# A Strassen projection in another order, with four of seven low halves of weights on GpSimd instead of five

## The chip, the cores and the metric

The kernel runs on one core of a Trainium2 chip. The metric is the time of one execution on the device in microseconds (us); smaller is better.

## The reference

One encoder layer over two sequences of 1024 and 512 tokens, 1536 in all, with 1024 channels, in float32. What the change touches is the first step, the projection of the normalised input to all branches:

```python
h = _rmsnorm(x, norm_pre)
p = h @ w_in
idx = [int(i) for i in np.cumsum(SPLIT_SIZES)[:-1]]
q_m, k_m, v_m, o_m, z_m, if_raw, q_a, k_a, v_a, z_a, g_m, g_a = jnp.split(p, idx, axis=-1)
```

`w_in` has 1024 rows and 9744 columns. The mLSTM branch, the grouped attention branch with a two-dimensional rotary embedding (rope) on q and k, the gates and the output projection follow.

## The kernel before

Four functions run one after the other, each behind a barrier of all engines: `project`, `attend`, `mlstm` and `finish`. Only `project` (from line 270) and the tables in front of it (lines 108 to 268) are touched.

**Products.** Float32 is multiplied as two parts of fp32r, high and low: hi x hi + hi x lo + lo x hi, three matmuls for each slice of 128 channels (lines 1063 to 1065). The matrix product is done by Strassen's scheme, in Winograd's form: activations and weights are cut in four blocks, and seven products of sums of blocks (A11, A12, S2, S3, S1, A22, S4, in this order) give the four corners. The tokens are done in two passes of 768. In each, 19 units of 512 columns of weights follow one another; a unit in a pass is called a run, 38 in all: 9 of a pass write p by tokens (three tiles of 256 columns to a product, four of them with gates, whose two halves are multiplied after sigmoid and silu), 10 by features (two tiles of 384 tokens). The first run of a pass is 8 columns wider, for the input and forget gates.

**One product.** SyncE loads the weights of a run in two halves (`raw`, three buffers). VectorE makes the weights' sums, called rest: S3 (line 725), S2 (731), S1 (733, in place) and A22 (737, in place). ScalarE rounds each to its high half (942, a ring of three slots, which waits until the product three before has ended), and GpSimd (611) or VectorE (741) subtracts it for the low half: GpSimd for A11, A12, S3, S1 and S4, VectorE for S2 and A22. TensorE multiplies tile by tile into one of two groups of three PSUM banks; before a product it waits until all of the product two before is evacuated. Each tile is evacuated by itself: A11 by ScalarE (948), the others by VectorE (752, 757, 771, 773), which adds it to what it has of the scheme in `parts` and writes corners to `stage`. ScalarE applies the gates' functions (953) and issues the stores. VectorE waits for the store of the run before ahead of the first tile of a corner.

**Activations.** Before a pass the input's tiles are normalised (ScalarE 918 and 923, VectorE 698, 704 and 708), the sums S1 to S4 are made by GpSimd (622 to 627) into one buffer `sums`, and 21 blocks of 128 tokens a pass are transposed by TensorE ("flip", 1039), rounded by ScalarE (929) and their low halves made by VectorE (715). In the first pass the flips are ordered by tile of tokens, then by block, and the last ones stand ahead of product S2 or S3 of run 0. For the second pass this work is laid between the products of runs 15 to 18, by way of DRAM.

**Rope.** While later units are multiplied, 12 tiles of q and k (six in runs 3 to 14, six in runs 22 to 35) are loaded, squared, normalised, turned by cosine (VectorE, 875) and sine (GpSimd, 646: four instructions), added (885), multiplied by the norm on GpSimd (653), split in high and low (ScalarE 1002 to 1004, VectorE 889 to 893), transposed on TensorE (1089) and copied out of PSUM alternately by ScalarE (1011) and VectorE (900).

**Order.** `project_plan` (line 172) gives every step a tick, where one tick is the time of one product; run r begins at tick 7r. Each engine takes its steps strictly in the order of their ticks, and semaphores alone make it wait:

```python
def at(engine, tick, kind, *n):
    plan[engine].append((tick, len(plan[engine]), kind, n))
```

The function `over_turns` and the product helper of line 101 belong to other stages.

Of the kernel before, what the change touches and what calls it, by code (L numbers as in the profile page):

```python
# [125 lines left out]
POOL_LOWS = (A11, A12, S3, S1, S4)  # L126
# [38 lines left out]
def flip_order():  # L165

    order = [(0, b, j) for j in range(HTT) for b in (A11, A12)]
    order += [(0, b, j) for j in range(HTT) for b in (S2, S3, S1, A22, S4)]
    return order + [(1, b, j) for b in range(PRODUCTS) for j in range(HTT)]


def project_plan():
# [17 lines left out]
    for j in range(HTT):  # L190
# [24 lines left out]
    for r in range(RUNS):  # L215
# [5 lines left out]
        at("dve", start - 0.9, "rest", r, S3)  # L221
        at("dve", start - 0.6, "rest", r, S2)
        at("dve", start + 1.2, "rest", r, S1)
        at("dve", start + 2.3, "rest", r, A22)
        n = HTT if tokens else 2
        for b in range(PRODUCTS):
            q = start + b
            at("act", q - 1.95, "high", r, b)
            at("pool" if b in POOL_LOWS else "dve", q - 1.6, "low", r, b)
            for i in range(n):  # L230
                at("pe", q + i / n, "product", r, b, i)
                at("act" if b == A11 else "dve", q + (i + 1) / n + 0.05, "out", r, b, i)
            if b in CORNERS:
                if funcs[0] is not ACT.Copy:
                    at("act", q + 1.3, "shape", r, b)
                if gated and b >= A22:
                    at("dve", q + 1.6, "gate product", r, b)
                if b >= A22:
                    at("act", q + (1.9 if gated else 1.4), "send", r, b)
# [11 lines left out]
    for t in range(TT):  # L251
        p = t // (2 * HTT)
        base, pace = ROPE_BASE[p] + ROPE_PACE[p] * (t % (2 * HTT)), ROPE_PACE[p] / 12
        for engine, tick, kind in (
                ("sp", 0.3, "load tile"), ("dve", 1.5, "tables"), ("act", 1.6, "rope square"), ("dve", 2.0, "sum squares"),
                ("act", 2.4, "rope root"), ("dve", 2.5, "cosine"), ("pool", 2.5, "sine"), ("dve", 2.9, "invert"),
                ("dve", 3.6, "add"), ("pool", 4.0, "rope normalise"), ("act", 4.7, "rope high"), ("dve", 5.4, "rope low"),
                ("sp", 6.3, "store v")):
            at(engine, base + pace * tick, kind, t)
        for f in range(RBANKS):  # L260
            tick = base + pace * (6.6 + 0.75 * f)
            at("pe", tick, "rope transpose", t, f)
            at("dve" if f % 2 else "act", tick + 0.3 * pace, "rope empty", t, f)
# [6 lines left out]
def project(nc, x, w_in, norm_pre, b_if, rope, q_gain, k_gain, p_feat, p_tok, stacks, v_stacks, neg_max, columns, bounce,  # L270
            blocks):

    with Scope(nc, "a") as sc:
# [15 lines left out]
        def room(first, *shape):  # L289
# [30 lines left out]
        acc = [[sc.pb(f"acc{g}{i}", [P, CH]) for i in range(HTT)] for g in range(2)]  # L320
# [4 lines left out]
        squared, mean_made, root_made, rstd_made, h_made, sums_made = (sc.sem(n) for n in (  # L325
            "squared", "mean_made", "root_made", "rstd_made", "h_made", "sums_made"))
# [39 lines left out]

        def unit_of_run(r):
# [11 lines left out]
        tiles_until = [sum(tiles(i) for i in range(r)) for r in range(RUNS + 1)]  # L379
# [8 lines left out]
        def full_count(r, b, i):  # L388
            return PRODUCTS * tiles_until[r] + b * tiles(r) + i + 1

        def out_count(r, b, i):

            if b == A11:
                return out_act, CREDIT + tiles_until[r] + i + 1
            return out_dve, CREDIT + (PRODUCTS - 1) * tiles_until[r] + (b - 1) * tiles(r) + i + 1

        def await_out(eng, r, b, i=None):
            eng.wait_ge(*out_count(r, b, tiles(r) - 1 if i is None else i))

        def low_count(r, b):  # L400

            mine = POOL_LOWS if b in POOL_LOWS else (S2, A22)
# [37 lines left out]
        def bank(r, b, i):  # L440
            return acc[(PRODUCTS * r + b) % 2][i]

        def part_of(which, r, i):

            w = width(r)
            return parts[:, which, i * w:(i + 1) * w]

        def place(r, b, i=None):

            lower_tokens, lower_cols = {A12: (True, True), S1: (False, False), A22: (False, True), S4: (True, False)}[b]  # L450
            if unit_of_run(r)[0]:
                s, edge_at = 0 if lower_tokens else 1, HALF - narrow(r) // 2
                cut = slice(0, edge_at) if lower_cols else slice(edge_at, 2 * HALF)
                v = stage[:, s, :].rearrange("p (n c) -> p n c", c=2 * HALF)[:, :, cut]
            else:
                s = 0 if lower_cols else 1
# [1779 lines left out]
```

## Time and profile before

| What | us |
|---|---|
| Median of three runs (2544.54 to 2550.89) | 2549.8 |
| The profiled execution, own time | 2546.88 |
| Its span from first to last instruction | 2544.8 |
| First product of the projection begins | 33.5 |
| Run 1 begins | 88.9 |
| Last matmul of the projection ends | 1319.4 |
| PE busy over the span (91%) | 2316.1 |
| DVE busy (65%) | 1657.7 |
| ACT busy (48%) | 1211.0 |
| POOL busy (45%) | 1139.5 |

In the profile PE is TensorE, PEld its load of weights, DVE VectorE, ACT ScalarE, POOL GpSimd and SP SyncE. Names of tiles carry the stage as first letter (`a_` is the projection), L and a number is a line of the kernel. Times in a trace count from the span's start. Matmuls overlap in their records, so the pace of PE is read from how many stand in a window, not from the mean duration of one. The clock in a window is the share of full speed granted to TensorE. A wait is idle time of an engine, with the instruction that ended it.

### The profile page before, as it was taken

The numbers are of one execution on the slowest core, as the hardware profiler recorded it, in microseconds if no ns is written. First come the engines' busy times: TensorE is split into PE (matmuls) and PEld (weight loads), VectorE is DVE, ScalarE is ACT, GpSimd is POOL, SyncE is SP. The second block draws the span as 40 slices with busy tenths as digits, with TensorE's granted clock in tenths as the row PEclk, the third lists the DMA queues.
The fourth block names the chain that finished last, engine by engine and source line by source line (L and its number), as shares of the span: only waits on it lengthen the run. The fifth ranks groups of instructions, "written<-read, shape, count | busy, mean of one in ns | idle before, by whom it ended". The sixth has DMA issues, their size and how long they took to land. (4 is left out here: it accounts for less than half of the span.)

```text
span 2544.8 us, 38884 instructions
## 1 busy us (share of the span) xinstructions
PE 2316.1 (91%) x14261; PEld 2121.3 (83%) x14261; DVE 1657.7 (65%) x2583; ACT 1211.0 (48%) x1976; POOL 1139.5 (45%) x626
## 2 busy tenths in 40 slices
PE   4999989998999999999978998989869995999998
PEld 4999989998899999999977777777668884888887
DVE  5567777765666778777638888888768872113222
ACT  4233553343443355334427877878667873211121
POOL 3454445545434544554426776767600002534420
PEclk9999999999999999999989999999989997999999
DMA  2334434455543333444424332221054434753332
GB/s 109 118 130 134 133 119 143 157 170 187 187 141 135 130 113 129 156 155 159 145 107 137 106 98 88 87 87 38 17 164 154 149 100 160 254 173 104 120 141 83
DMA packets 203462, 331.93 MB, mean 130 GB/s; under 512 B 10288, under 2 KB 96144, under 8 KB 203280
## 3 DMA queue, kind: packets, MB, share of 16 engines
q1 hardware_dynamic: 177712, 275.57, 33.4%
q10 hardware_dynamic: 25568, 54.01, 5.5%
q8 instruction: 104, 1.70, 0.3%
q14 instruction: 78, 0.64, 0.1%
HBM read 223.18 MB, written 106.37 MB: 129 GB/s over the span
## 5 line engine op out<-in xcount | busy, mean ns | idle before, releaser
L611 POOL TENSOR_TENSOR a_w_lo<-a_raw,a_w_hi 128x1024 fp32r<-128x1024 f32 (+1 forms) x152 | 397.7, 2619 | 364.2 <-ACT a_w_hi L942 364.2
L1063 PE MATMUL a_acc<-a_w_hi,a_act_hi 128*128 128x256 f32 (+1 forms) x1512 | 438.0, 290 | 26.6 <-DVE a_stage L771 11.7
L1064 PE MATMUL a_acc<-a_w_lo,a_act_hi 128*128 128x256 f32 (+1 forms) x1512 | 432.8, 286 | 0.0
L1065 PE MATMUL a_acc<-a_w_hi,a_act_lo 128*128 128x256 f32 (+1 forms) x1512 | 432.6, 286 | 0.0
L1063 PE MATMUL a_acc<-a_act_hi,a_w_hi 128*128 128x384 f32 x1120 | 386.1, 345 | 38.8 <-POOL a_w_lo L611 14.4
L942 ACT ACTIVATE a_w_hi<-a_raw 128x1024 fp32r<-128x1024 f32 (+1 forms) x190 | 201.5, 1061 | 423.6 <-PE a_acc L1065 381.8
L1065 PE MATMUL a_acc<-a_act_hi,a_w_lo 128*128 128x384 f32 x1120 | 379.3, 339 | 0.0
L1064 PE MATMUL a_acc<-a_act_lo,a_w_hi 128*128 128x384 f32 x1120 | 378.7, 338 | 0.0
L1763 POOL TENSOR_TENSOR t_prob<-t_prob,t_rsum 128x1024 f32<-128x1024 f32 (+1 forms) x192 | 308.2, 1609 | 124.2 <-DVE t_rsum L1783 124.1
L1063 PEld LDWEIGHTS a_acc<-a_w_hi,a_act_hi 128*128 128x128 f32 x1512 | 294.5, 195 | 30.1 <-issue 21.3
L771 DVE TENSOR_TENSOR a_stage<-a_parts,a_acc 128x256 f32<-128x256 f32 (+3 forms) x376 | 172.8, 471 | 225.0 <-PE a_acc L1065 201.7
L1064 PEld LDWEIGHTS a_acc<-a_w_lo,a_act_hi 128*128 128x128 f32 x1512 | 294.6, 195 | 0.0
L1065 PEld LDWEIGHTS a_acc<-a_w_hi,a_act_lo 128*128 128x128 f32 x1512 | 294.4, 195 | 0.0
L1063 PEld LDWEIGHTS a_acc<-a_act_hi,a_w_hi 128*128 128x128 f32 x1120 | 213.6, 191 | 46.1 <-issue 27.6
L2066 POOL TENSOR_TENSOR f_w_lo<-f_raw,f_w_hi 128x512 fp32r<-128x512 f32 x48 | 63.7, 1357 | 358.7 <-ACT f_w_hi L2082 358.7
L1779 DVE TENSOR_REDUCE t_nmax<-t_scr 128x1 f32<-128x1024 f32 (+1 forms) x192 | 199.2, 1037 | 34.2 <-PE t_scr L1842 34.1
L1789 DVE TENSOR_TENSOR t_pt_lo<-t_flip,t_pt_hi 128x512 fp32r<-128x512 f32 x320 | 206.7, 679 | 18.2 <-issue 10.6
L1064 PEld LDWEIGHTS a_acc<-a_act_lo,a_w_hi 128*128 128x128 f32 x1120 | 214.2, 191 | 0.0
L1065 PEld LDWEIGHTS a_acc<-a_act_hi,a_w_lo 128*128 128x128 f32 x1120 | 213.5, 191 | 0.0
L1810 ACT ACTIVATE t_prob<-t_scr,t_nmax 128x1024 f32<-128x1024 f32 (+1 forms) x192 | 187.5, 977 | 48.6 <-DVE t_nmax L1779 32.7
L1842 PE MATMUL t_scr<-t_k,t_q 128*128 128x512 f32 x640 | 184.1, 402 | 28.7 <-DMA t_k<-stacks 19.2
L611 POOL TENSOR_TENSOR a_w_lo<-a_rest,a_w_hi 128x1024 fp32r<-128x1024 f32 (+1 forms) x38 | 96.9, 2550 | 248.8 <-ACT a_w_hi L942 248.7
(214 smaller groups left out, 5168.6 us busy)
## 6 DMA issues: line engine op xcount, KB each, us to landing
a_raw<-w_in SPq DMA_DIRECT2D x56, 1024.0 KB, 5.3
p_feat<-a_stage ACTq DMA_DIRECT2D x40, 768.0 KB, 3.5
stacks<-a_guest SPq DMA_DIRECT2D x72, 256.0 KB, 2.6
a_raw<-w_in SPq DMA_DIRECT2D x32, 512.0 KB, 4.7
p_tok<-a_stage ACTq DMA_DIRECT2D x20, 768.0 KB, 3.5
t_q<-stacks SPq DMA_DIRECT2D x8, 1536.0 KB, 6.6
t_k<-stacks SPq DMA_DIRECT2D x16, 768.0 KB, 9.1
m_raw<-p_feat SPq DMA_DIRECT2D x24, 512.0 KB, 4.0
```

The source lines that it names most:

```text
L611: nc.gpsimd.tensor_sub(slot_of(w_lo, r, b), weights_of(r, b), slot_of(w_hi, r, b).bitcast(F32))\
L771: ins = nc.vector.tensor_add(out, known[:, skip:w], a[:, skip:w])
L942: nc.scalar.activation(slot_of(w_hi, r, b), weights_of(r, b), ACT.Copy).then_inc(hi_made, 1)
L1063: nc.tensor.matmul(out, s_hi, m_hi, start=begin, stop=False)
L1064: nc.tensor.matmul(out, s_hi, m_lo, start=False, stop=False)
L1065: last = nc.tensor.matmul(out, s_lo, m_hi, start=False, stop=end)
L1763: nc.gpsimd.tensor_mul(prob[n % 3][:, 0:w], prob[n % 3][:, 0:w], rsum[:, 1, n % 4:n % 4 + 1].to_broadcast([P, w])).then_inc(normed, 1)
L1779: nc.vector.tensor_reduce(out=nmax[:, n % 4:n % 4 + 1], in_=scr[n % 2][:, 0:w], axis=AX.X, op=ALU.max, negate=True).then_inc(max_made, 1)
L1789: nc.vector.tensor_sub(pt_lo[b][place(m, i)], flip[x % FLIPS][:], pt_hi[b][place(m, i)].bitcast(F32)).then_inc(lo_made[x % FLIPS], 1)
L1810: nc.scalar.activation(prob[n % 3][:, 0:w], scr[n % 2][:, 0:w], ACT.Exp, bias=nmax[:, n % 4:n % 4 + 1], accum_out=rsum[:, 0, n % 4:n % 4 + ...
L1842: ins = nc.tensor.matmul(scr[n % 2][:, i * CH:(i + 1) * CH], q_t[s][:, hd % 2, q * P:(q + 1) * P], k_t[s][:, part, keys], start=(part == 0 ...
L2066: nc.gpsimd.tensor_sub(w_lo[cut], raw[:, k % (KT // 2), :], w_hi[cut].bitcast(F32))\
```

## The change

- GpSimd computes four of a run's seven low halves, VectorE three: S4 moves.
- All tiles of a product are evacuated by one instruction, over a tensor of three banks, after the product's last matmul. Semaphores count products, not tiles.
- The rests of a run are ordered 0.8 to 1.6 ticks earlier.
- The two stage buffers change roles after each token run (`swapped`), so that the first corner of a run goes to the buffer whose store was issued first.
- In the first pass VectorE makes the sums S1 to S4, into buffers of their own for each tile; S3 and S4 overwrite input tiles that are no longer needed. Flips are ordered by block, each block just ahead of its product. The flips of A11 and A12 stand 0.25 tick later, and the high halves of the first two weights 0.55 tick earlier.
- Rope's cosine, sine, norm and low steps are cut in smaller steps, with more ticks between them; ScalarE does all copies of its transposes.

The diff, cut to its core:

```diff
-POOL_LOWS = (A11, A12, S3, S1, S4)
+POOL_LOWS, DVE_LOWS = (A11, A12, S3, S1), (S2, A22, S4)
...
-    order += [(0, b, j) for j in range(HTT) for b in (S2, S3, S1, A22, S4)]
+    order += [(0, b, j) for b in (S2, S3, S1, A22, S4) for j in range(HTT)]
...
-            flip(0, b, j, -3.3 + 0.4 * j + 0.08 * i)
-        token_tile(HTT + j, -1.2 + 0.4 * j)
-        at("pool", 0.3 + 0.4 * j, "sums", 0, j)
+            flip(0, b, j, -3.05 + 0.4 * j + 0.08 * i)
+        token_tile(HTT + j, -1.2 + 0.3 * j)
         for i, b in enumerate((S2, S3, S1, A22, S4)):
-            flip(0, b, j, (1.9, 2.2, 2.5)[j] + 0.02 * i)
+            if b not in (S1, A22):
+                at("dve", i + 0.05 + 0.1 * j, "first sums", b, j)
+            flip(0, b, j, 1.7 + i + 0.1 * j)
...
-        at("dve", start - 0.9, "rest", r, S3)
-        at("dve", start - 0.6, "rest", r, S2)
-        at("dve", start + 1.2, "rest", r, S1)
-        at("dve", start + 2.3, "rest", r, A22)
+        at("dve", start - 1.7, "rest", r, S3)
+        at("dve", start - 1.4, "rest", r, S2)
+        at("dve", start - 0.2, "rest", r, S1)
+        at("dve", start + 0.7, "rest", r, A22)
...
-            at("act", q - 1.95, "high", r, b)
+            at("act", q - 1.95 if q > 1 else q - 2.5, "high", r, b)
             at("pool" if b in POOL_LOWS else "dve", q - 1.6, "low", r, b)
             for i in range(n):
                 at("pe", q + i / n, "product", r, b, i)
-                at("act" if b == A11 else "dve", q + (i + 1) / n + 0.05, "out", r, b, i)
+            at("act" if b == A11 else "dve", q + 1.05, "out", r, b)
...
-                ("act", 2.4, "rope root"), ("dve", 2.5, "cosine"), ("pool", 2.5, "sine"), ("dve", 2.9, "invert"),
-                ("dve", 3.6, "add"), ("pool", 4.0, "rope normalise"), ("act", 4.7, "rope high"), ("dve", 5.4, "rope low"),
-                ("sp", 6.3, "store v")):
+                ("act", 2.4, "rope root"), ("dve", 2.9, "invert"), ("dve", 4.2, "add"),
+                ("act", 5.9, "rope high"), ("sp", 7.0, "store v")):
             at(engine, base + pace * tick, kind, t)
+        for i in range(2):
+            at("dve", base + pace * (2.5 + 0.7 * i), "cosine", t, i)
+            for h in range(2):
+                at("pool", base + pace * (2.2 + 0.8 * h + 0.4 * i), "sine", t, i, h)
+            at("pool", base + pace * (4.5 + 0.7 * i), "rope normalise", t, i)
+            at("dve", base + pace * (6.2 + 0.5 * i), "rope low", t, i)
         for f in range(RBANKS):
-            tick = base + pace * (6.6 + 0.75 * f)
+            tick = base + pace * (7.2 + 0.75 * f)
             at("pe", tick, "rope transpose", t, f)
-            at("dve" if f % 2 else "act", tick + 0.3 * pace, "rope empty", t, f)
+            at("act", tick + 0.3 * pace, "rope empty", t, f)
...
-        acc = [[sc.pb(f"acc{g}{i}", [P, CH]) for i in range(HTT)] for g in range(2)]
+        acc = [sc.pb(f"acc{g}", [P, HTT, CH]) for g in range(2)]
...
+        swapped = [sum(unit_of_run(i)[0] for i in range(r)) % 2 for r in range(RUNS)]
...
+        def bank(r, b):
+            return acc[(PRODUCTS * r + b) % 2][:, 0:tiles(r), 0:width(r)]
...
+            s = (s + swapped[r]) % 2
+            return s, stage[:, s, :].rearrange("p (n c) -> p n c", c=c)[:, :, cut]
...
+                    elif kind == "first sums":
+                        b, j = n
+                        upper, lower = xt[j], xt[HTT + j]
+                        if b == S2:
+                            dve.wait_ge(h_made, CREDIT + 2 * HTT)
+                            nc.vector.tensor_add(first_sum(S1, j), lower[:, 0:CH], lower[:, CH:D]).then_inc(first_sums, 1)
+                            dve.wait_ge(first_sums, CREDIT + first_sum_no(S1, j))
+                            nc.vector.tensor_sub(first_sum(S2, j), first_sum(S1, j), upper[:, 0:CH]).then_inc(first_sums, 1)
+                        elif b == S3:
+                            dve.wait_ge(flipped, CREDIT + flip_no[0, A11, j] + 1)
+                            dve.wait_ge(first_sums, CREDIT + first_sum_no(S2, j))
+                            nc.vector.tensor_sub(first_sum(S3, j), upper[:, 0:CH], lower[:, 0:CH]).then_inc(first_sums, 1)
+                        elif b == S4:
+                            dve.wait_ge(flipped, CREDIT + flip_no[0, A12, j] + 1)
+                            nc.vector.tensor_sub(first_sum(S4, j), upper[:, CH:D], first_sum(S2, j)).then_inc(first_sums, 1)
...
                         elif b == S3:
-                            await_out(dve, r, S2, i)
-                            if r and i == 0:
-                                await_out(dve, r - 1, A22)
-                            nc.vector.tensor_add(u3, p1, a[:, 0:w]).then_inc(out_dve, 1)
+                            await_out(dve, r, S2)
+                            nc.vector.tensor_add(u3, p1, a).then_inc(out_dve, 1)
...
-                        last.then_inc(acc_full, 1)
+                        if i == tiles(r) - 1:
+                            last.then_inc(acc_full, 1)
```

## Rows read from the trace of the kernel before

**Rows 1.** Stage windows: length; busy PE, PEld, DVE, ACT, POOL; clock; DMA.

```profile
33.40:179.60 146.20, 136.18 (x1068) 133.25 (x1069) 91.33 (x143) 46.78 (x68) 74.81 (x42) 0.96 0.28 97
179.60:560.80 381.20, 353.52 (x2414) 348.59 (x2413) 286.62 (x360) 161.62 (x193) 189.63 (x82) 0.98 0.44 144
560.80:672.70 111.90, 96.27 (x507) 93.57 (x506) 67.54 (x79) 50.66 (x75) 56.94 (x28) 0.92 0.45 158
672.70:834.10 161.40, 160.45 (x1266) 159.74 (x1265) 105.90 (x203) 63.16 (x84) 63.09 (x25) 1.00 0.47 164
834.10:1261.00 426.90, 408.95 (x2751) 404.55 (x2751) 322.76 (x406) 189.71 (x224) 219.35 (x95) 0.98 0.42 141
1261.00:1319.40 58.40, 58.38 (x337) 58.06 (x335) 30.08 (x40) 20.61 (x24) 20.20 (x8) 1.00 0.21 77
```

**Rows 2.** Windows of single runs without a wait, same columns.

```profile
119.13:149.37 30.24, 30.24 (x255) 30.24 (x253) 16.91 (x28) 8.36 (x10) 12.44 (x5) 1.00 0.36 123
461.20:492.20 31.00, 31.00 (x187) 30.85 (x186) 18.53 (x22) 10.53 (x12) 12.32 (x5) 1.00 0.71 225
1040.00:1069.10 29.10, 29.10 (x170) 29.10 (x169) 24.18 (x31) 10.95 (x12) 17.68 (x9) 1.00 0.55 182
```

**Rows 3.** Waits of PE, 60 to 1320 us: total us, times, longest.

```profile
PE a_acc L1063 <- DVE a_stage L771: 25.7, 16, 3.1
PE a_acc L1063 <- POOL a_w_lo L611: 16.9, 9, 3.9
PE a_acc L1063 <- DVE a_parts L773: 7.6, 3, 5.3
PE a_acc L1063 <- DVE a_parts L752: 5.9, 4, 2.4
PE a_acc L1063 <- DVE a_parts L757: 3.6, 3, 2.2
...
PE a_acc L1063 <- ACT a_parts L948: 1.4, 4, 0.6
```

**Rows 4.** Waits of PE, 560.8 to 672.7 us, runs 15 to 17.

```profile
PE a_acc L1063 <- POOL a_w_lo L611: 11.7, 3, 3.9
PE a_acc L1063 <- DVE a_stage L771: 3.1, 3, 1.0
PE a_acc L1063 <- ACT a_parts L948: 0.8, 3, 0.3
```

**Rows 5.** Timeline of run 4 on DVE and POOL: start, us, instruction.

```profile
180.74 2.96 DVE L731 TENSOR_TENSOR a_rest<-a_rest,a_raw 128x1024 f32<-128x1024 f32 x1
...
179.23 3.38 POOL L611 TENSOR_TENSOR a_w_lo<-a_raw,a_w_hi 128x1024 fp32r<-128x1024 f32 x1
```

**Rows 6.** Line 731: minimum, median, maximum ns.

```profile
L731 DVE TENSOR_TENSOR a_rest<-a_rest,a_raw x38: 1211/3098/3311, 37.9 to 1287.9; 128x1024 f32<-128x1024 f32 x36, 128x1056 f32<-128x1056 f32 x2
```

**Rows 7.** Lines of DVE by form in the projection: busy us, mean ns.

```profile
L771 DVE TENSOR_TENSOR a_stage<-a_parts,a_acc 128x384 f32<-128x384 f32 x160 | 85.8, 548 | 124.4 <-PE a_acc L1065 118.7 <-DMA p_tok<-a_stage 3.3 <-DMA p_feat<-a_stage 2.4
...
L771 DVE TENSOR_TENSOR a_stage<-a_parts,a_acc 128x256 f32<-128x256 f32 x192 | 77.2, 414 | 95.7 <-PE a_acc L1065 78.2 <-DMA p_tok<-a_stage 17.4
...
L741 DVE TENSOR_TENSOR a_w_lo<-a_raw,a_w_hi 128x1024 fp32r<-128x1024 f32 x36 | 54.2, 1506 | 7.5 <-ACT a_w_hi L942 7.5
```

**Rows 8.** Lines of POOL by form in the projection.

```profile
L611 POOL TENSOR_TENSOR a_w_lo<-a_raw,a_w_hi 128x1024 fp32r<-128x1024 f32 x144 | 376.8, 2619 | 324.3 <-ACT a_w_hi L942 324.3
```

**Rows 9.** DMA issues, part 6 of the page: KB each, us to landing.

```profile
a_raw<-w_in SPq DMA_DIRECT2D x56, 1024.0 KB, 5.3
```

**Rows 10.** Waits of DVE, whole projection.

```profile
DVE a_stage L771 <- DMA p_tok<-a_stage: 20.7, 9, 4.5
```

**Rows 11.** Timeline of PE in the head.

```profile
22.56 1.97 PE L1039 MATMUL a_flip<-a_ident,a_guest 128*128 128x128 f32 x8 [3.80 <-DVE a_guest L708]
...
33.47 0.59 PE L1063 MATMUL a_acc<-a_w_hi,a_act_hi 128*128 128x264 f32 x1 [4.17 <-POOL a_w_lo L611]
```

**Rows 12.** Timeline of POOL in run 15.

```profile
580.98 4.66 POOL L611 TENSOR_TENSOR a_w_lo<-a_raw,a_w_hi 128x1024 fp32r<-128x1024 f32 x2
```

More of the change, by code:

```diff
@@ L365, in project, with first_sum, first_sum_no @@
         PER_PASS = PRODUCTS * HTT
+        def first_sum(b, j):
+            if b in (S3, S4):
+                return xt[j][:, 0:CH] if b == S3 else xt[j][:, CH:D]
+            return sums[:, j, :] if b == S2 else room(2 * HTT * D + (HTT + j) * CH, CH)
+        def first_sum_no(b, j):
+            return {S1: 2 * j + 1, S2: 2 * j + 2, S3: 2 * HTT + j + 1, S4: 3 * HTT + j + 1}[b]
         def unit_of_run(r):
@@ L438, in slot_of, with part_of, place @@
             return tile[:, (PRODUCTS * r + b) % RING, 0:KH * s].rearrange("p (k c) -> p k c", k=KH)[:, :, 0:half_columns(r)]
[L440 to L448, printed above, removed]
+        def bank(r, b):
+            return acc[(PRODUCTS * r + b) % 2][:, 0:tiles(r), 0:width(r)]
+        def part_of(which, r):
+            return parts[:, which, 0:tiles(r) * width(r)].rearrange("p (n w) -> p n w", w=width(r))
+        def place(r, b):
             lower_tokens, lower_cols = {A12: (True, True), S1: (False, False), A22: (False, True), S4: (True, False)}[b]
@@ L757, in _ @@
[L757 to L759 removed]
+                            await_out(dve, r, S2)
+                            nc.vector.tensor_add(u3, p1, a).then_inc(out_dve, 1)
                         else:
[L761 removed]
+                            await_out(dve, r, S1 if b == S4 else S3)
                         if b in CORNERS:
[L763 removed]
+                            s, out = place(r, b)
@@ L771, in _ @@
-                            ins = nc.vector.tensor_add(out, known[:, skip:w], a[:, skip:w])
+                                t = 2 * HTT * (r // NPROJ) + (HTT if b == A22 else 0)
+                                nc.vector.tensor_add(gate_tok[:, t:t + HTT, :], known[:, :, 0:skip], a[:, :, 0:skip])\
+                                    .then_inc(gates_added, 1)
+                            ins = nc.vector.tensor_add(out, known[:, :, skip:], a[:, :, skip:])
                             if b == S1:
-                                ins = nc.vector.tensor_add(p1, p1, a[:, 0:w])
+                                ins = nc.vector.tensor_add(p1, p1, a)
@@ L956, in _ @@
                         tokens, _, (f1, f2), where = unit_of_run(r)
-                        s = sent_at(r, b)
+                        part = sent_at(r, b)
+                        s = (part + swapped[r]) % 2
                         if f1 is ACT.Copy:
@@ L966, in _ @@
                             cols_out = 2 * HALF if f1 is f2 else HALF
-                            rows = p_tok[first + HT * s:first + HT * (s + 1), where:where + cols_out]
+                            rows = p_tok[first + HT * part:first + HT * (part + 1), where:where + cols_out]
                             act.dma_start(rows.rearrange("(n p) c -> p n c", p=P),
@@ L971, in _ @@
                         else:
-                            rows = p_feat[where + HALF * s:where + HALF * (s + 1), first:first + PT]
+                            rows = p_feat[where + HALF * part:where + HALF * (part + 1), first:first + PT]
                             act.dma_start(rows.rearrange("(n p) t -> p n t", p=P),
@@ L997, in _ @@
                         t = n[0]
[L998 removed]
+                        act.wait_ge(normed, CREDIT + 2 * t + 2)
                         if t:
```

140 lines of the change are left out of this document (59 added, 81 removed).

## The prediction

> **What bounds the kernel now.** I read the stage windows first. The diff touches only the projection, the work up to 1319.4 us; the stages behind it start after its barrier and keep their time. In the projection TensorE is busy nearly throughout (353.5 of 381.2 us in one stretch), and the granted clock dips to 0.92 in one [rows 1]. So the question is how far TensorE stands above its undisturbed pace.
>
> That pace stands in three windows of single runs [rows 2]. A run is seven products. A token run takes 30.24 us, 4.32 a product; a feature run takes 29.1 us, 4.16 a product; a feature run with 187 matmuls in place of 168 (the 19 are transposes of rope) takes 31.0, so a transpose costs 0.1 us. I call one product a tick. The excess of a stretch is its length less its runs at this pace and less its transposes:
> - Runs 0 to 3 (60 flip transposes): 146.2 - 4 x 30.24 - 6 = 19.2 us.
> - Runs 4 to 14, five token and six feature runs, with rope (144 transposes): 381.2 - 151.2 - 174.6 - 14.4 = 41.0 us.
> - Runs 15 to 17, which make the sums of the second pass: 111.9 - 87.3 = 24.6 us.
> - Runs 18 to 22 (84 flip transposes): 161.4 - 29.1 - 121.0 - 8.4 = 2.9 us.
> - Runs 23 to 35, five and eight, with rope: 426.9 - 151.2 - 232.8 - 14.4 = 28.5 us.
>
> The waits of TensorE's products explain it: 61.1 us in 39 waits after 60 us [rows 3], 15.6 us in 9 of them in runs 15 to 17 [rows 4]. That leaves 45.5 us in 30 waits for the two rope stretches, against 69.5 us of excess. The clock explains most of the rest: 0.98 granted over 381 and 427 us is about 16 us lost [rows 1]. One rope wait therefore costs 69.5 / 30 = 2.3 us with all that follows it.
>
> Most of them end with VectorE, at evacuations (lines 771, 752, 757, 773), not with GpSimd. VectorE works in order, so I looked at what stands ahead of a late evacuation. In run 4 the rest sum of line 731 takes 2.96 us, while GpSimd computes a low half for 3.38 us over the same time [rows 5]. The same sum takes 1211 to 3311 ns over the kernel, with a median of 3098 [rows 6]. So a sum of two SBUF tensors on VectorE is held up while GpSimd runs, and the evacuations queue behind it. Rope adds clumps: four sines back to back on GpSimd, and four low steps back to back on VectorE.
>
> **The change part by part.** *Evacuations merged.* The two widths, 414 ns at 256 elements and 548 at 384 [rows 7], give 1.05 ns an element and 146 ns fixed. Seven VectorE evacuations a run become one instruction where they were three (18 token runs) or two (20 feature runs): 18 x 7 x 2 + 20 x 7 = 392 fewer, 57 us of VectorE. By the Trainium skill ("VectorE: DVE Perf Modes", the TRN2 errata section) a PSUM source has 120 cycles fixed, an estimate of 125 ns and 49 us; the row decides, and neither reaches the time, since it is cover, not path. The price is that a tile no longer leaves while the next one is multiplied. An evacuation of 768 elements takes 146 + 768 x 1.05 = 0.95 us after the product, where the last tile took 0.41 or 0.55. TensorE needs it one product (4.2 us) later, so it is hidden unless VectorE is late; only at the very end does it cost 0.4 us.
>
> *Low half of S4 to VectorE.* 38 x 1.51 us = 57 us more there [rows 7], 38 x 2.62 = 100 us less on GpSimd [rows 8]. GpSimd holds VectorE up less often. The chain for S4 itself becomes shorter. The odd rope copies (three a tile) go from VectorE to ScalarE, busy 161.6 of 381.2 us in the first rope stretch [rows 1]; I cost them at nothing and leave out what VectorE saves by them. The first pass's sums (12 of 512 elements) come onto VectorE, about 0.15 + 512 x 1.05 = 0.68 us each, 8 us in all. VectorE's total is nearly unchanged: -57 + 57 + 8 = 8 us, less the rope copies.
>
> *Rests 0.8 to 1.6 ticks earlier; rope in smaller steps further apart; stage buffers swapped.* These change the order only. Rest S3 moves from 0.9 to 1.7 ticks before its run, 7.1 us. Its second half of weights is issued 4.0 ticks ahead, 16.6 us, and lands 5.3 us later [rows 9], 11.3 us ahead: 4 us to spare. Earlier rests also free ScalarE, whose high half of S2 has to wait for line 731. Swapping removes most of 20.7 us in which VectorE stood before an evacuation until a store had landed [rows 10]; part of that is in the rope excess already.
>
> What goes and what is late next: rope still brings the VectorE steps of 12 tiles, which must pass between evacuations. The gain is bounded by 0 and the whole 69.5 us. I let each tile keep one wait at 2.3 us: 12 x 2.3 = 28 stay, **41 us go** (a choice, not a row). I take a value above the middle because both the clumps and the locked sums ahead of evacuations, shown in [rows 5], are what the new ticks pull apart.
>
> *The head.* TensorE starts its first product at 33.47 us [rows 11]; the second tile's transposes waited 3.80 us for a norm that stood behind the first tile's low halves on VectorE. With the flips 0.25 tick later the norms go first. Moving the norm by the two low halves and their ScalarE steps, for two tiles, is worth up to 7 us. In run 0 the flips then go product by product, and the sums no longer wait for a shared buffer; but norms, rests and sums now share VectorE in front of S2. I take 8 us for head and run 0 together, between -6 (VectorE becomes the chain) and 15.
>
> *Runs 15 to 17.* GpSimd still makes four sums in front of S1's low half (at 580.98 us, with no idle time behind the last sum) [rows 12], and TensorE waits 3.9 us for it [rows 4]. Nothing there moves: 0, between -3 and 6.
>
> Sum: 8 + 41 + 0 - 0.4 = 48.6 us. The profiled execution took 2546.9 us (its span 2544.8 and 2.1 around it): 2498.3. The runs' median lies 2.9 above it, so the forecast is **2501 us**.
>
> **Rivals.**
> - *Nearly all of the rope excess goes* (0.17). For it: runs 36 and 37, without rope, have all of the weights' work and keep the pace, 58.4 us [rows 1]. 2546.9 - 8 - 69.5 + 0.4 + 2.9 = 2473, and down to 2466 if the head gives 15.
> - *The clumps only move* (0.14). VectorE's total stays, so an in-order engine may be late as often. Then the head is all that is left: 2542, and 2550 without it. Against it: the waits stand at few places and not evenly over the runs.
> - *Slower: two locked rests in front of A22's evacuation* (0.13). In the new order VectorE does between the end of product S1 and the evacuation of A22, which has to be done two products (8.3 us) later: two merged sums for S1 (1.9), rest S3, rest S2, and A22's own 0.95. With both rests free (1.21 each [rows 6]) that is 1.9 + 2.42 + 0.95 = 5.3 us; with one held to the median of 3.1, 7.2; with both, 9.05, which is 0.75 too late. It decides from the point where both are locked in over half of the runs: at 2.3 us a wait, 21 runs eat up the 48.6. In 34 of 38 runs it is 78 us: 2501 + 78 = 2579. For it: GpSimd's low half of A11 falls just there, and each late run invites the next lock. Against it: a low half is 2.62 of 4.2 us [rows 8], so GpSimd is idle between A11's and A12's for about 1.5 us, enough for one free rest of 1.21. The Trainium skill ("Perfetto Trace Analysis", Matmuls) wants independent groups to rotate through PSUM banks so that evacuation overlaps the next group; by that rule three banks freed at once would be the worse choice, this rival's direction. The trace of before has no such case.
>
> **How the numbers follow.** Forecast 0.56, its own range 2485 to 2522. 0.3% is 7.6 us and about what a measurement of this kernel can tell from no change, so faster is below 2542. Of the clumps case I count half as faster and half as same; 0.02 of the forecast lies at same. Faster 0.54 + 0.17 + 0.07 = 0.78, same 0.07 + 0.02 = 0.09, slower 0.13. The range leaves out the lower end of the first rival and the slower one beyond a few late runs: 2468 to 2550.
>
> **What would show it.** Right: TensorE's waits for evacuations in the rope runs fall from 30 to about 12; line 731's median falls towards 1.2 us while line 725, now over A11's low half, may take up its delay; the wait for the store before an evacuation is gone; run 1 begins near 81 us in place of 88.9; runs 15 to 17 keep their 3.9 us waits. Wrong: a wait of TensorE at A11 in most runs, with both rests long in front of it, or a VectorE wait for the weights' landing.

## The result, and the profile after

The changed kernel takes 2521.97 us, the median of 4 runs (2515.87 to 2526.39); the kernel before takes 2547.3 us on the same chip. The ratio is 0.9898, with a 95% interval of 0.9871 to 0.9925: 1.0% faster, some 25 us, where 48.6 were forecast. The median lies 0.03 us inside the upper end of the forecast's own range (2485 to 2522), and two of the four runs lie above it. The profiled execution took 2523.8 us over a span of 2521.7, against 2546.9 before, 23.1 less.

The stages give these 23 us. The view is that of busy time by stretch, with the bounds moved to where the same runs begin in the new trace: length; busy PE, PEld, DVE, ACT, POOL; granted clock; DMA share; GB/s. The first line is run 0 alone, the second runs 1 to 3, which stand as one line in [rows 1]; the other five are the stages of [rows 1].

```profile
25.90:85.20 59.30, 44.44 (x312) 42.62 (x313) 44.84 (x54) 20.99 (x39) 13.78 (x5) 0.88 0.15 51
85.20:178.60 93.40, 90.88 (x758) 90.67 (x756) 56.52 (x50) 25.90 (x26) 33.83 (x18) 1.00 0.35 125
178.60:549.70 371.10, 352.04 (x2413) 348.33 (x2414) 268.66 (x240) 170.52 (x195) 167.50 (x79) 0.97 0.44 147
549.70:656.30 106.60, 93.64 (x505) 90.94 (x504) 76.00 (x61) 51.03 (x72) 47.65 (x25) 0.95 0.47 166
656.30:820.20 163.90, 160.89 (x1268) 160.09 (x1267) 108.09 (x141) 62.28 (x75) 49.55 (x21) 1.00 0.47 162
820.20:1237.50 417.30, 404.69 (x2751) 401.84 (x2750) 302.17 (x275) 196.39 (x225) 189.26 (x88) 0.99 0.43 144
1237.50:1295.90 58.40, 58.36 (x337) 58.04 (x335) 30.05 (x26) 20.69 (x22) 14.87 (x7) 1.00 0.22 82
```

| Stretch | before, us | after, us | gain |
|---|---|---|---|
| up to the first product | 33.5 | 25.9 | +7.6 |
| run 0 | 55.4 | 59.3 | -3.9 |
| runs 1 to 3 | 90.7 | 93.4 | -2.7 |
| runs 4 to 14 (rope) | 381.2 | 371.1 | +10.1 |
| runs 15 to 17 | 111.9 | 106.6 | +5.3 |
| runs 18 to 22 | 161.4 | 163.9 | -2.5 |
| runs 23 to 35 (rope) | 426.9 | 417.3 | +9.6 |
| runs 36 and 37 | 58.4 | 58.4 | 0 |

The rope stretches gave 19.7 us, and 9.1 of what was won went back in run 0 and in two stretches that had nearly kept the pace before. What TensorE waits for has changed its kind. From 60 us to the projection's end, in us, times, longest:

```profile
PE a_acc L1076 <- DVE a_stage L788: 23.8, 17, 3.8
PE a_flip L1103 <- DVE a_guest L912: 15.5, 7, 4.9
PE a_acc L1076 <- POOL a_w_lo L622: 9.3, 3, 3.1
PE a_flip L1052 <- DVE a_act_lo L722: 4.1, 3, 1.9
PE a_acc L1076 <- ACT a_parts L960: 0.7, 3, 0.2
PE a_acc L1076 <- DVE a_parts L773: 0.6, 1, 0.6
```

Against [rows 3], the waits for evacuations (788, 773) are 18 in place of 26 (lines 771, 773, 752, 757), 24.4 us in place of 42.8. The second row is new: TensorE stands before rope's transposes until VectorE has made the last low half of the tile. It takes back most of what the first row and GpSimd gave: 15.5 of 26.0 us.

In the two rope stretches alone (from 0.1 us behind their first product), the first two rows below are runs 4 to 14 and the last two runs 23 to 35:

```profile
PE a_flip L1103 <- DVE a_guest L912: 12.4, 6, 4.9
PE a_acc L1076 <- DVE a_stage L788: 8.3, 5, 3.0
...
PE a_acc L1076 <- DVE a_stage L788: 9.6, 7, 3.8
PE a_flip L1103 <- DVE a_guest L912: 3.0, 1, 3.0
```

With one of 0.6 us at line 773 these are 20 waits, 13 of them at evacuations. The rope stretches had 30, and not all of these were at evacuations: 6 of the 9 waits for GpSimd in [rows 3] lie there too.

The rests' durations by line show what VectorE was held up in (minimum, median, maximum ns):

```profile
L747 DVE TENSOR_TENSOR a_rest<-a_raw x38: 1212/2942/3196, 25.6 to 1260.2; 128x1024 f32<-128x1024 f32 x36, 128x1056 f32<-128x1056 f32 x2
...
L753 DVE TENSOR_TENSOR a_rest<-a_rest,a_raw x38: 1210/1225/3392, 27.0 to 1263.2; 128x1024 f32<-128x1024 f32 x36, 128x1056 f32<-128x1056 f32 x2
...
L755 DVE TENSOR_TENSOR a_raw<-a_raw x38: 1210/2278/3421, 35.4 to 1265.2; 128x1024 f32<-128x1024 f32 x36, 128x1056 f32<-128x1056 f32 x2
```

The rest of S2 is now free in its median (3098 ns in [rows 6]); those of S3 (as the prediction thought possible) and S1 are held up in theirs, and were free before:

```profile
L725 DVE TENSOR_TENSOR a_rest<-a_raw x38: 1211/1219/3517, 32.4 to 1286.6; 128x1024 f32<-128x1024 f32 x36, 128x1056 f32<-128x1056 f32 x2
...
L733 DVE TENSOR_TENSOR a_raw<-a_raw x38: 1211/1218/3429, 45.8 to 1293.4; 128x1024 f32<-128x1024 f32 x36, 128x1056 f32<-128x1056 f32 x2
```

Where such a rest meets a step of rope ahead of A22's evacuation, TensorE waits. This is VectorE, then GpSimd, then TensorE at the end of run 3: start, us, instruction.

```profile
170.84 1.23 DVE L747 TENSOR_TENSOR a_rest<-a_raw 128x1024 f32<-128x1024 f32 x1
172.10 2.21 DVE L753 TENSOR_TENSOR a_rest<-a_rest,a_raw 128x1024 f32<-128x1024 f32 x1
174.23 3.41 DVE L891 TENSOR_TENSOR a_guest<-a_guest,a_tab 128x1024 f32<-128x1024 f32 x1
177.56 0.94 DVE L788 TENSOR_TENSOR a_stage<-a_parts,a_acc 128x768 f32<-128x768 f32 x1
...
170.84 2.38 POOL L653 TENSOR_TENSOR a_guest<-a_guest,a_tab 128x512 f32<-128x512 f32 x1 [12.73 <-DVE a_rope_stat L880]
173.19 3.37 POOL L622 TENSOR_TENSOR a_w_lo<-a_raw,a_w_hi 128x1024 fp32r<-128x1024 f32 x1
...
178.65 0.35 PE L1076 MATMUL a_acc<-a_w_hi,a_act_hi 128*128 128x256 f32 x1 [2.57 <-DVE a_stage L788]
```

Rest S3, rest S2 and rope's cosine stand one behind the other; the last two meet GpSimd at work, and the evacuation begins at 177.56. The 2.57 us are nearly the whole 2.7 that runs 1 to 3 lost.

### The profile page after: what moved, and what is told of

Its sections match the earlier page's. It is cut to its first block and busy times, and to the rows that moved or that the text cites. A ratio compares the mean times of both kernels' runs of the same rounds, so it can differ in the third digit from the quotient of the medians.

```text
span 2521.7 us, 38165 instructions
## 1 busy us (share of the span) xinstructions
PE 2308.0 (92%) x14261; PEld 2116.5 (84%) x14261; DVE 1639.5 (65%) x2197; ACT 1225.0 (49%) x1956; POOL 1032.4 (41%) x588
## 5 line engine op out<-in xcount | busy, mean ns | idle before, releaser
L622 POOL TENSOR_TENSOR a_w_lo<-a_raw,a_w_hi 128x1024 fp32r<-128x1024 f32 (+1 forms) x114 | 288.4, 2529 | 412.0 <-ACT a_w_hi L954 411.8
L788 DVE TENSOR_TENSOR a_stage<-a_parts,a_acc 128x768 f32<-128x768 f32 (+2 forms) x152 | 144.1, 948 | 165.6 <-PE a_acc L1078 165.5
L1076 PEld LDWEIGHTS a_acc<-a_act_hi,a_w_hi 128*128 128x128 f32 x1120 | 213.5, 191 | 26.5 <-issue 15.8
L1824 ACT ACTIVATE t_prob<-t_scr,t_nmax 128x1024 f32<-128x1024 f32 (+1 forms) x192 | 187.7, 978 | 49.3 <-DVE t_nmax L1793 33.5
L1865 PE MATMUL t_flip<-t_ident,t_prob 128*128 128x128 f32 x1280 | 183.9, 277 | 25.6 <-DVE t_pt_lo L1803 25.3
```

The costliest lines, as they stand in the source:

```text
L622: nc.gpsimd.tensor_sub(slot_of(w_lo, r, b), weights_of(r, b), slot_of(w_hi, r, b).bitcast(F32))\
L788: ins = nc.vector.tensor_add(out, known[:, :, skip:], a[:, :, skip:])
L1076: nc.tensor.matmul(out, s_hi, m_hi, start=begin, stop=False)
L1824: nc.scalar.activation(prob[n % 3][:, 0:w], scr[n % 2][:, 0:w], ACT.Exp, bias=nmax[:, n % 4:n % 4 + 1], accum_out=rsum[:, 0, n % 4:n % 4 + ...
L1865: ins = nc.tensor.transpose(flip[x % FLIPS][:, j, :], prob[n % 3][:, (4 * i + j) * P:(4 * i + j + 1) * P], ident[:])
```

## The experiments

Times are medians, ratios to the kernel before of the same chip; where a kernel is compared with the changed kernel, the latter is 2521.97 us, 0.9898 [0.9871, 0.9925]. Not all ran on one chip; the kernel before took 2545.18 to 2547.54 us on the chips of the experiments, so a difference of a few us between two rows is read with the ratios and the stages beside it.

| Run | What | us | ratio, interval |
|---|---|---|---|
| e1 | rope's transposes later | 2509.84 | 0.9862, 0.9846 to 0.9879 |
| e2 | rests at their old ticks | 2519.7 | 0.9903, 0.9887 to 0.992 |
| e3 | low half of S4 on GpSimd | 2523.7 | 0.991, 0.9894 to 0.9927 |
| e4 | rope at its old ticks | 2539.12 | 0.9966, 0.9951 to 0.9981 |
| e5 | before, with the head's ticks alone | 2538.99 | 0.9973, 0.9962 to 0.9984 |
| e6 | e1, rests S3 and S2 earlier still | 2516.2 | 0.9883, 0.9866 to 0.9899 |
| e7 | e1, sums of the second pass behind S1's low half | 2497.77 | 0.9808, 0.9792 to 0.9824 |
| e8 | stage buffers not swapped | 2520.04 | 0.989, 0.9873 to 0.9906 |
| e9 | e7, rests at their old ticks | 2482.03 | 0.9745, 0.9729 to 0.9762 |
| e10 | e7, rest S2 alone behind A22's evacuation | 2482.03 | 0.974, 0.9723 to 0.9756 |
| e11 | evacuations split again | 2528.15 | 0.9927, 0.9911 to 0.9944 |

### e1: rope's transposes a product later

```diff
-            tick = base + pace * (7.2 + 0.75 * f)
+            tick = base + pace * (8.2 + 0.75 * f)
```

> The changed kernel with the rope transposes one twelfth of a tile's pace later (8.2 in place of 7.2; their copies and stores follow). Theory: seven new waits of TensorE for the last rope low step (15.5 us, line 912) took back part of the rope gain, and each also costs clock; they go and nothing else takes their place, so 13 to 25 us below the changed kernel's 2522, that is 2497 to 2509. Rival: VectorE is late for whatever comes next, so the waits turn up before evacuations, and the time stays within 2517 to 2527.

Measured: 2509.84 us, just above the theory's 2509. Runs 4 to 14 alone became shorter, 371.1 to 357.9 us; runs 23 to 35 stayed (417.7). TensorE's waits from 60 us to the end:

```profile
PE a_acc L1076 <- DVE a_stage L788: 29.2, 20, 3.8
...
```

and its window of runs 4 to 14:

```profile
178.60:536.50 357.90, 348.13 (x2413) 345.58 (x2414) 263.94 (x240) 169.27 (x195) 168.67 (x79) 0.99 0.46 152
```

The 7 waits at line 1103 are gone, and 5.4 us of waits for evacuations came in their place. Besides the waits, the same 2413 matmuls took 3.9 us less of busy time than in the changed kernel (348.13 and 352.04), at a granted clock of 0.99 in place of 0.97. Six of the seven waits lay in this stretch; in the other, one wait of 3.0 us went and 2.0 us of waits for evacuations came. So the rival was right in part. The trace of the changed kernel shows how such a wait comes about, VectorE first:

```profile
442.18 2.95 DVE L747 TENSOR_TENSOR a_rest<-a_raw 128x1024 f32<-128x1024 f32 x1
445.16 1.23 DVE L753 TENSOR_TENSOR a_rest<-a_rest,a_raw 128x1024 f32<-128x1024 f32 x1
446.30 3.42 DVE L907 TENSOR_TENSOR a_guest<-a_guest 128x1024 f32<-128x1024 f32 x1
449.65 0.94 DVE L788 TENSOR_TENSOR a_stage<-a_parts,a_acc 128x768 f32<-128x768 f32 x1
...
451.30 0.43 DVE L912 COPY a_guest<-a_guest 128x512 f32<-128x512 f32 x1
...
451.78 0.69 PE L1103 MATMUL a_flip<-a_ident,a_guest 128*128 128x128 f32 x2 [3.05 <-DVE a_guest L912]
```

Two rests, the first low step (held up to 3.42 us) and an evacuation stand ahead of the last low step. TensorE's wait begins at 448.73 and that evacuation ends at 450.59, so some 1.9 of the 3.05 us could stay when the transposes are moved away, which is how waits for evacuations came in e1. The diff allowed for less: from the low step to the transpose there were 1.2 steps of rope's pace (5.4 to 6.6), and now 0.5 (6.7 to 7.2).

### e2: the rests at their old ticks

```diff
-        at("dve", start - 1.7, "rest", r, S3)
-        at("dve", start - 1.4, "rest", r, S2)
-        at("dve", start - 0.2, "rest", r, S1)
-        at("dve", start + 0.7, "rest", r, A22)
+        at("dve", start - 0.9, "rest", r, S3)
+        at("dve", start - 0.6, "rest", r, S2)
+        at("dve", start + 1.2, "rest", r, S1)
+        at("dve", start + 2.3, "rest", r, A22)
```

> The changed kernel with the four weight sums (rests) back at their old ticks. Theory: the early rests stand behind GpSimd's low half of A11 and in front of A22's evacuation, so TensorE's waits at A11 and A12 (about 19 us in 13 waits in the changed kernel) go, but line 753 is held up again as before and ScalarE waits for it; net between 2512 and 2530. Rival, that the early rests are what brought the rope gain: 2535 or more.

Measured: 2519.7 us, no difference that the intervals can tell. Yet the stages moved: run 0 from 59.3 to 54.5, runs 1 to 3 to 91.4, runs 18 to 22 to 161.5, all near or at what they were before, while runs 15 to 17 rose from 106.6 to 114.1. Its waits of TensorE:

```profile
PE a_flip L1103 <- DVE a_guest L912: 21.1, 8, 7.6
PE a_acc L1076 <- POOL a_w_lo L622: 19.5, 9, 5.0
PE a_acc L1076 <- DVE a_stage L788: 8.4, 7, 1.8
```

The waits for evacuations at line 788 fall from 23.8 to 8.4 us, those for the transposes and for GpSimd rise by 15.8. So the earlier rests did cost something at the evacuations, but two other waits hid it. In runs 15 to 17 the three waits for GpSimd are 14.9 us in place of 9.3. Line 753 is long again here (median 3306 ns), and ScalarE waits for it, 107.8 us in 27 times; outside runs 15 to 17 TensorE's waits for GpSimd rise from none to 4.6 us in 6, and whether that is its price was not tested. In run 0 the rest of S2 now comes behind the first norm and that of S1 behind most of the sums, instead of ahead of norms: the last norm ends at 35.1 instead of 38.0 us.

### e3, e8 and e11: what was costed at nothing

```diff
-POOL_LOWS, DVE_LOWS = (A11, A12, S3, S1), (S2, A22, S4)
+POOL_LOWS, DVE_LOWS = (A11, A12, S3, S1, S4), (S2, A22)
```

> The changed kernel with the low half of S4 back on GpSimd. Theory: moving it hardly matters for the time, since VectorE takes 1.4 us more and is held up less by GpSimd: 2517 to 2529. Rival, that GpSimd's share is what held VectorE up: 2532 to 2545, with medians of the rests near 3 us. A second rival, that it loads VectorE in its full stretch: below 2515.

```diff
-        swapped = [sum(unit_of_run(i)[0] for i in range(r)) % 2 for r in range(RUNS)]
+        swapped = [0 for r in range(RUNS)]
```

> The changed kernel without the exchange of the two stage buffers. Theory: VectorE's wait for stores ahead of A12's evacuation comes back in the gated token runs (20.7 us in 9 waits before), and part of it reaches TensorE there: 2524 to 2534. Rival, that the wait is cover: 2519 to 2524.

```diff
-                            ins = nc.vector.tensor_add(out, known[:, :, skip:], a[:, :, skip:])
+                            for i in range(tiles(r)):
+                                ins = nc.vector.tensor_add(out[:, i, :], known[:, i, skip:], a[:, i, skip:])
```

(and the other three evacuations of VectorE alike)

> The changed kernel with each merged evacuation of 768 elements issued as its single evacuations of 256 again, one behind the other at the same place behind the product. Theory A (the merge is cover: VectorE has idle time around it, only the place counts): 2520 to 2528, the same waits. Theory B (the fixed part of an instruction, 146 ns each by 952 and the three of before, is on the path, since VectorE is what evacuations wait for): VectorE busier by some 50 us, 2530 to 2545. Theory C (a bank that comes free earlier lets the next product start earlier): below 2516.

Measured: 2523.7, 2520.04 and 2528.15 us. The first two are within 2 us of the changed kernel, as e3's theory and e8's rival had it. Without the swap VectorE waits for a store again, and nothing became slower:

```profile
DVE a_stage L788 <- DMA p_tok<-a_stage: 15.5, 4, 7.0
```

e11 lies just above the 2528 that its first theory allowed, and below the second's 2530; it is 6 us above the changed kernel, 7 by the ratios, and the intervals overlap, so the merge may be worth that much or nothing. The reason that it is little is in the size. Three evacuations of 256 behind one another in e11, and one of 768 in the changed kernel:

```profile
237.95 1.07 DVE L793 TENSOR_TENSOR a_stage<-a_parts,a_acc 128x256 f32<-128x256 f32 x3
```

```profile
236.48 0.94 DVE L788 TENSOR_TENSOR a_stage<-a_parts,a_acc 128x768 f32<-128x768 f32 x1
```

Two instructions fewer save 0.13 us, 65 ns each, not 146: records of neighbours overlap. By the windows VectorE's busy time in the projection is 901.6 us in e11 and 886.3 in the changed kernel, 15 us and not 57.

### e4 and e5: rope undone, and the head alone

e4 takes the changed kernel and puts cosine, sine, add, norm, high, low and transposes of rope back at their old ticks (ScalarE keeps the copies, and the steps stay cut in smaller instructions):

```diff
-            at("dve", base + pace * (6.2 + 0.5 * i), "rope low", t, i)
+            at("dve", base + pace * 5.4, "rope low", t, i)
...
-            tick = base + pace * (7.2 + 0.75 * f)
+            tick = base + pace * (6.6 + 0.75 * f)
```

> The changed kernel with rope's steps back at the old ticks (all copies stay on ScalarE). Theory: the clumps are what made TensorE wait for evacuations in the rope runs, so those waits come back while the waits for the transposes go: 2525 to 2545. Rival, that merged evacuations and the order of the rests brought the gain: 2505 to 2520.

e5 takes the kernel before and changes the head's ticks alone:

```diff
-            flip(0, b, j, -3.3 + 0.4 * j + 0.08 * i)
-        token_tile(HTT + j, -1.2 + 0.4 * j)
+            flip(0, b, j, -3.05 + 0.4 * j + 0.08 * i)
+        token_tile(HTT + j, -1.2 + 0.3 * j)
...
-            at("act", q - 1.95, "high", r, b)
+            at("act", q - 1.95 if q > 1 else q - 2.5, "high", r, b)
```

> The kernel before with nothing but the ticks of the head changed (flips of A11 and A12 0.25 later, the second set of tiles closer, the first two high halves earlier). Theory: the first product starts at 26 us instead of 33.5, as in the changed kernel, because a norm no longer stands behind low halves; the sums stay on GpSimd, so run 0 is not lengthened and all of it reaches the end: 2537 to 2542. Rival, that VectorE's sums and the flips by block are needed as well: S2 of run 0 starts where it did, and the time is 2544 to 2549.

Measured: 2539.12 and 2538.99 us, the same. So the change without rope's new ticks is worth about its head, 7.6 us (2546.57 to 2538.99 on that chip): merged evacuations, S4's low half, the swap, the earlier rests, the copies on ScalarE and run 0's sums come to nothing together. That nothing is a sum. By its windows e4, against the kernel before, gains 7.7 us in runs 15 to 17 and 2.6 in runs 4 to 14, and loses 4.9 in run 0, 2.4 in runs 1 to 3, 2.7 in runs 18 to 22 and 2.4 in runs 23 to 35. Rope's ticks are worth 17 us (2539.12 less 2521.97). In e4 runs 4 to 14 take 378.6 us and runs 23 to 35 429.3; TensorE's waits for evacuations are 41.7 us in 23 there (lines 788, 790 and 773), about the 42.8 in 26 of [rows 3].

### e6: rests earlier still

```diff
-        at("dve", start - 1.7, "rest", r, S3)
-        at("dve", start - 1.4, "rest", r, S2)
+        at("dve", start - 2.5, "rest", r, S3)
+        at("dve", start - 2.2, "rest", r, S2)
```

(with e1's edit)

> The changed kernel with the later rope transposes of e1 and rests S3 and S2 at 2.5 and 2.2 ticks ahead of their run, in front of product S1's evacuation, where GpSimd has no low half since S4's moved away. Theory: A22's evacuation no longer stands behind a held-up rest, so TensorE's waits at A11 and A12 (about 29 us in 20 waits in e1) fall by more than half, the median of line 747 falls to 1.2 us, and the time is 2485 to 2500. Rival: the weights land too late for it and VectorE waits for them with evacuations behind it: 2510 or more, with a wait of VectorE for the load.

Measured: 2516.2 us, 6 more than e1, as the rival had it; the intervals of the two overlap. TensorE's first wait, and a new one of VectorE's:

```profile
PE a_acc L1076 <- DVE a_parts L790: 26.3, 10, 3.3
```

```profile
DVE a_rest L747 <- DMA a_raw<-w_in: 16.7, 4, 5.7
```

Its runs 15 to 17 are the line

```profile
538.40:653.70 115.30, 95.81 (x506) 93.11 (x505) 73.87 (x60) 49.99 (x72) 47.77 (x25) 0.94 0.47 166
```

The rest of S3 is free here (median 1218 ns), as are the other three (1225, 1218 and 1218), and VectorE's busy time in the projection is 824.3 us, where it is 881.9 in e1. The waits for line 788 fall to 5.0 us; but now the rests stand ahead of S1's evacuation (788 and 790), and TensorE waits for that one instead. The loss lies in runs 15 to 17: they are 9.6 us longer than e1's, with 16.3 of the 16.7 us in which VectorE stood until the weights had landed, and the other stretches together are 3.3 us shorter than in e1.

### e7: the sums of the second pass behind S1's low half

```diff
-        at("pool", base + 2.8, "sums", 1, j)
+        at("pool", base + 3.45, "sums", 1, j)
```

(with e1's edit)

> e1 with the second pass's sums on GpSimd behind the low half of S1 instead of in front of it (0.65 tick later). Theory: TensorE's 3.1 us wait in each of runs 15 to 17 goes, with its loss of clock, so the stretch falls from 106 to about 93 us and the time to 2495 to 2501. Rival: the sums hold up another low half or the loads of x, and the stretch stays above 102.

Measured: 2497.77 us, 12.1 below e1. GpSimd in run 15 of the changed kernel:

```profile
566.80 2.13 POOL L635 TENSOR_TENSOR a_guest<-a_guest 128x512 f32<-128x512 f32 x1
568.90 2.34 POOL L622 TENSOR_TENSOR a_w_lo<-a_raw,a_w_hi 128x1024 fp32r<-128x1024 f32 x1
```

As in [rows 12] the low half of S1 begins where the last sum ends, and TensorE waits 3.1 us three times. In e7 the sums come behind it, and the stage is the line

```profile
534.10:626.70 92.60, 88.96 (x507) 87.22 (x506) 70.40 (x61) 51.06 (x72) 53.45 (x25) 1.00 0.57 198
```

It is 14.0 us shorter than the changed kernel's (13.1 shorter than e1's), where the three waits were 9.3. The rest is the clock: the same matmuls (505 and 507 records) take 88.96 us of busy time at a granted clock of 1.00, all of it at 2.4 GHz, in place of 93.64 at 0.95. Two shorter windows of the changed kernel, around the first of the three waits, show it:

```profile
566.00:571.40 5.40, 2.26 (x14) 1.94 (x12) 4.82 (x3) 1.06 (x1) 5.16 (x3) 0.89 0.00 0
571.40:576.00 4.60, 4.60 (x15) 4.60 (x16) 0.93 (x1) 0.00 (x0) 0.00 (x0) 0.50 0.76 177
```

TensorE stood for 3.14 of the first 5.4 us, and the 4.6 us behind were granted 0.50, the level of 1.2 GHz.

### e9 and e10: which rest makes A11 wait

e9 is e7 with e2's edit; e10 moves one rest of e7:

```diff
-        at("dve", start - 1.4, "rest", r, S2)
+        at("dve", start - 0.9, "rest", r, S2)
```

Where these two expectations speak of S1's evacuation, S1's low half is meant, as in e7.

> Kernel e7 (rope's transposes a product later, second pass's sums behind S1's evacuation) with the rests of the a columns back at their places of before (-0.9, -0.6, +1.2, +2.3). Theory A (the new places of the rests cost more than they gain, as e2 showed: run 0 4.8 us shorter, runs 1 to 3 2.0, fewer waits for evacuations): the gain adds to e7's, run 0 near 54, runs 1 to 3 near 91, runs 4 to 14 near 355, waits for a_stage below 10 us in sum: 2482 to 2492. Theory B (with the two other waits gone the rests' places are cover, or the sums behind S1's evacuation now collide with a rest at +1.2): within 4 us of e7, 2494 to 2502, or worse, with waits for A22's or A12's operands in place of those for evacuations.

> Kernel e7 with only the rest of S2 put back behind A22's evacuation (-0.9), the rest of S3 left at its new place ahead of it. Theory A (two rests held up one behind the other ahead of A22's evacuation are what A11 waits for; one alone is hidden): the waits of A11 go, and nothing is late for S2: 2484 to 2494, near e9. Theory B (it is the rest of S3, which is the one held up since the change, that makes the wait): waits at A11 stay, 2494 to 2500.

Measured: both 2482.03 us, 15.7 below e7 (16 and 17 by the ratios), 65 below the kernel before; e10 is 2 us below the range of its theory A. The waits for line 788 in e9 are 12.4 us, where below 10 were expected. The two rope stretches of e9 and of e10:

```profile
172.40:529.90 357.50, 345.28 (x2413) 341.42 (x2414) 262.95 (x239) 169.11 (x195) 178.01 (x80) 1.00 0.46 150
...
785.00:1197.20 412.20, 403.90 (x2751) 400.68 (x2750) 307.91 (x275) 197.76 (x224) 199.40 (x89) 1.00 0.44 145
```

```profile
174.00:528.80 354.80, 345.40 (x2413) 342.70 (x2414) 266.37 (x240) 169.46 (x195) 174.14 (x80) 1.00 0.47 153
...
785.50:1196.90 411.40, 403.45 (x2751) 400.55 (x2750) 310.39 (x274) 198.83 (x224) 190.96 (x89) 1.00 0.43 145
```

With one rest moved by half a product, e10 gains what e9 gains with four. The rest of S3 stays long in it (line 747, median 2942 ns), so one held-up rest ahead of A22's evacuation is mostly hidden, and it is the second one that is too much. The end of run 3 in e10, on VectorE, beside the same place shown above:

```profile
168.26 1.22 DVE L747 TENSOR_TENSOR a_rest<-a_raw 128x1024 f32<-128x1024 f32 x1
169.40 2.32 DVE L891 TENSOR_TENSOR a_guest<-a_guest,a_tab 128x1024 f32<-128x1024 f32 x1
171.64 0.94 DVE L788 TENSOR_TENSOR a_stage<-a_parts,a_acc 128x768 f32<-128x768 f32 x1
172.51 2.54 DVE L753 TENSOR_TENSOR a_rest<-a_rest,a_raw 128x1024 f32<-128x1024 f32 x1
```

From the rest of S3 to the evacuation it is 3.4 us here and was 6.7. Runs 1 to 3 and 18 to 22 take 91.4 and 162.2 us. Not all waits went: those at line 788 fell from 29.7 us in e7 to 17.3 in e10. The longest there, 3.32 us, comes from the next evacuation, that of S4, which begins at 1137.40: the rest of S2, both cosine steps and the rest of S1 (3.23 us) stand ahead of it.

## Why the prediction was right in direction and wrong in size

- **The time.** 2521.97 lies inside the range by 0.03 us, and two changes that stood at nothing in the sum, 5.3 us won in runs 15 to 17 and 5.2 lost in runs 1 to 3 and 18 to 22, cancel. That it falls inside is luck; the terms have to be read one by one.
- **The head, 8 us with run 0.** The head itself was right: the first product begins at 25.95 in place of 33.47 us, and e5 shows the 7.6 us alone. Run 0 gave half of it back. The prediction named the cause (norms, rests and sums share VectorE in front of S2) and set it too low: run 1 begins at 85.2, not near 81. By e2 it is the earlier rests, not the sums: with them at their old ticks run 0 takes 54.5 us.
- **Rope, 41 of 69.5 us.** This is the step that failed. By the same reckoning the excess of the changed kernel is 30.9 us in runs 4 to 14 and 18.9 in runs 23 to 35, 49.8 together: 19.7 us went. The choice to "let each tile keep one wait at 2.3 us" counted the clumps pulled apart and not what they were moved towards. The price held, 49.8 us in 20 waits or 2.5 each; the number did not. At evacuations 13 waits are left, near the 12 (16 in e1, where no wait for a transpose hides any), and 7 at the transposes are new. Two things were in the diff and not in the sum. The transposes were moved 0.6 step later and the last low step 1.3, so that the transposes became a wait (e1: 12 us, all of it in runs 4 to 14). And the rest of S2 was moved ahead of A22's evacuation (e10 against e7: 15.7 us in all, and 8.1 in the rope stretches of the profiled executions, which differ by 9.4). With both undone, e10's excess is 14.6 + 13.0 = 27.6 us, about the 28 that were to stay, in 14 waits of 17.7 us; the mechanism was there, and two new waits took half of its worth. That it comes so near to 28 is in part chance, as the 28 was a choice and e10 also has e7's edit.
- **Stretches without rope at nothing.** Runs 1 to 3 and 18 to 22 lost 5.2 us. The earlier rests were held to "change the order only", with 4 us to spare for the weights. That was right for the weights (no wait for their landing in the changed kernel; it comes with e6), but the cover of A22's evacuation was priced under a rival only, and not here.
- **Runs 15 to 17 at 0, between -3 and 6.** 5.3 us came. The wait for GpSimd stayed, as forecast, though at 3.1 in place of 3.9 us (2.4 us for the three), and TensorE's busy time fell by 2.6 us at a clock of 0.95 in place of 0.92. Why the wait became shorter was not tested. That it is worth 13 to 14 us with the clock is shown by e7; the prediction saw the cause and read 11.7 us of waits from it.
- **Costed at nothing: merge, S4's low half, swap.** Right for the last two (e3, e8); for the merge, e11 leaves room for 6 to 7 us. The evacuation of 768 elements was set at 0.95 us, and 236.48 shows 0.94. The 57 us of VectorE were a wrong use of durations, and did not enter the sum.
- **The rivals.** "The clumps only move" falls with e4: rope's ticks do bring 17 us. "Nearly all of the rope excess goes" did not happen, nor in any run here. "Two locked rests" had the right place and the wrong frequency. Its condition, both long in over half of the runs, was not met: line 753 stayed at 1225 in its median while line 747 rose to 2942. One long rest alone is mostly hidden; where rope or the other rest joins it, A11 waits, in part of the runs.
- **The rule on PSUM banks** of the Trainium skill ("Perfetto Trace Analysis", Matmuls), which the prediction set beside that rival, is not tested: both kernels use two groups of three banks in turn, and e11 issues its pieces behind the product too. What the runs show is that a kernel that frees three banks at once reaches 2482 us.

## What to carry to other kernels

When steps are moved apart, count for every moved step what now stands between it and the one that waits for it, on the in-order engine that makes it: a gap of so many ticks on paper is worth nothing if two held-up sums and an evacuation fit into it. In these runs one long step ahead of an evacuation with a deadline was mostly hidden, and the second made TensorE wait. And when undoing a part of a change moves the total by nothing, look at the stages before calling it neutral: e2's edit gained in four places and lost in two, and was worth 15.7 us once the other two waits were gone.

## What the runs showed of the hardware that was not expected

- A wait of TensorE can cost more than its length. The one of 2.57 us in runs 1 to 3 cost 2.7, at a granted clock of 1.00. In runs 15 to 17, 9.3 us of waits for GpSimd were worth 14.0 us, 4.7 of it busy time at a lower granted clock (0.95 against 1.00); over runs 4 to 14 the same 2413 matmuls took 352.0 us at 0.97, 348.1 at 0.99 and 345.4 at 1.00. The prediction knew of 16 us for both rope stretches, but spread them over the waits there and gave the runs 15 to 17 none.
- The delay of VectorE behind GpSimd belongs to the place in the order and not to the instruction. The long rest was S2's (3098 ns), then S3's (2942) and S1's (2278), in e2 S2's again (3306); in e6, with S3 and S2 still earlier, all four are free in their medians (1218 to 1225). The Trainium skill ("SBUF — State Buffer", Who interferes with whom) says that a VectorE instruction with two SBUF inputs contends with a GpSimd instruction that reads SBUF, the later one being blocked; the trace agrees, with some 1.2 us for such an instruction of 1024 elements that is not held up, and 3.41 for the one that begins at 174.23 above, while GpSimd is at its low half from 173.19 to 176.56.
- The fixed part of an evacuation that follows another is about 65 ns, not the 146 by which the records of one grow: a duration's intercept is no price for an instruction in a row.
